# Scoring 24 of 128 expert tiles in the routing and table stages, and interleaving scores with outputs on TensorE

## What is computed

```python
q = (t @ wq).reshape(PEER_BLOCK, PEER_HEADS, 2, PEER_DQ // 2)
s1, s2 = einsum(q[:, :, 0], k1), einsum(q[:, :, 1], k2)
v1, i1 = lax.top_k(s1, 16); v2, i2 = lax.top_k(s2, 16)
score, ci = lax.top_k(v1[..., :, None] + v2[..., None, :], 16)
expert = i1[ci // 16] * 128 + i2[ci % 16]
g = softmax(score)
act = gelu(einsum('thkd,td->thk', u_tab[expert], t))
out = einsum('thk,thkd->td', g * act, v_tab[expert])
```

## Time and profile before

| | us |
|---|---|
| median of 3 runs (4811.25 to 4816.73) | 4812.54 |
| profiled execution | 4815.9 |
| its span, first to last instruction | 4814.1 |
| PE busy in it | 4348.4 (90%) |
| DVE busy | 2663.7 (55%) |
| ACT busy | 1814.3 (38%) |
| POOL busy | 526.0 (11%) |
| mean granted PE clock | 0.961 |

### The profile page before, as it was taken

How to read it: one execution, slowest core, us unless ns; L and a number is a source line. 1 busy time by engine, 2 the same in 40 slices (tenths; PEclk the granted TensorE clock), 3 DMA queues, 4 the chain that set the end, 5 groups by cost and what they waited for, 6 DMA issues and landing times. The chain is left out here.

```text
span 4814.1 us, 56280 instructions
## 1 busy us (share of the span) xinstructions
PE 4348.4 (90%) x20979; PEld 3540.2 (74%) x20979; DVE 2663.7 (55%) x4645; ACT 1814.3 (38%) x2539; POOL 526.0 (11%) x308
## 2 busy tenths in 40 slices
PE   8988888879998367999999997999999999999998
PEld 6866765646874256999999995777878877777887
DVE  0777758773437897767677675334343333434332
ACT  1665654443421033333333333345232233643322
POOL 0000000000003502334333430000000000000000
PEclk9999999989999699999999998999999999999999
DMA  7111101103322037887787771211323322122332
GB/s 263 58 40 44 40 31 49 43 1 108 92 63 67 5 140 281 281 279 270 282 278 276 274 273 65 70 53 59 99 88 97 96 84 70 51 77 84 102 97 81
DMA packets 196090, 579.09 MB, mean 120 GB/s; under 512 B 17345, under 2 KB 66753, under 8 KB 194369
## 3 DMA queue, kind: packets, MB, share of 16 engines
q1 hardware_dynamic: 158032, 435.34, 27.4%
q0 software_dynamic: 36864, 134.23, 7.9%
q10 hardware_dynamic: 1008, 7.03, 0.4%
HBM read 549.27 MB, written 27.26 MB: 120 GB/s over the span
## 5 line engine op out<-in xcount | busy, mean ns | idle before, releaser
L402 DVE TENSOR_TENSOR tile_rest<-tile_raw,tile_up 128x1024 fp32r<-128x1024 f32 (+2 forms) x288 | 338.7, 1181 | 786.4 <-ACT tile_up L393 786.2
L410 PE MATMUL layer_psum<-hn_up,tile_up 128*128 128x512 f32 x1344 | 534.7, 398 | 21.5 <-DVE hn_rest L497 21.5
L411 PE MATMUL layer_psum<-hn_up,tile_rest 128*128 128x512 f32 x1344 | 527.7, 393 | 0.0
L412 PE MATMUL layer_psum<-hn_rest,tile_up 128*128 128x512 f32 x1344 | 527.3, 392 | 0.0
L393 ACT ACTIVATE tile_up<-tile_raw 128x1024 fp32r<-128x1024 f32 (+2 forms) x288 | 291.4, 1018 | 370.3 <-PE layer_psum L412 368.5
L2205 PE MATMUL ex_psum<-ex_t_up,ex_u_up 128*128 128x384 f32 x1024 | 344.5, 336 | 9.1 <-ACT ex_prod L2280 4.9
L2207 PE MATMUL ex_psum<-ex_t_rest,ex_u_up 128*128 128x384 f32 x1024 | 344.4, 336 | 0.0
L2206 PE MATMUL ex_psum<-ex_t_up,ex_u_rest 128*128 128x384 f32 x1024 | 343.9, 336 | 0.0
L410 PEld LDWEIGHTS layer_psum<-hn_up,tile_up 128*128 128x128 f32 x1344 | 255.7, 190 | 82.4 <-issue 30.0
L2225 PE MATMUL ex_psum<-ex_v_up,ex_prod_rest 128*128 128x512 f32 x768 | 300.0, 391 | 0.0
L2223 PE MATMUL ex_psum<-ex_v_rest,ex_prod_up 128*128 128x512 f32 x768 | 299.9, 390 | 0.0
(11 more groups left out here) (450 smaller groups left out, 9981.3 us busy)
## 6 DMA issues: line engine op xcount, KB each, us to landing
ex_u<-in_peer_u SPq DMA_DIRECT2D x128, 512.0 KB, 4.3
tT<-in_peer_v SPq DMA_DIRECT2D x128, 512.0 KB
tile_raw<-in_w_gu SPq DMA_DIRECT2D x88, 512.0 KB, 3.6
xT<-in_w_head SPq DMA_DIRECT2D x56, 512.0 KB, 3.6
mod_w<-in_w_ada SPq DMA_DIRECT2D x48, 512.0 KB, 4.7
mg_w_raw<-in_w_merge SPq DMA_DIRECT2D x48, 512.0 KB
expert_table<-et_rows SPq DMA_DIRECT2D x6, 4096.0 KB
ex_rows<-expert_table SPq DMA_DIRECT2D x64, 384.0 KB, 6.2
```

The lines of the kernel that those rows point to most:

```text
L402: self.nc.vector.tensor_tensor(out=self.rest[:, n % self.SLOTS, 0:blocks, :], in0=self.raw[n % self.RAWS][:, 0:blocks, :], in1=self.up[:, ...
L410: self.nc.tensor.matmul(dst, w_up, up, start=first, stop=False)
L411: self.nc.tensor.matmul(dst, w_rest, up, start=False, stop=False)
L412: return self.nc.tensor.matmul(dst, w_up, rest, start=False, stop=last)
```

## The change

Every 5.33rd tile of the 128 (`EARLY`: 2, 8, 13, 18, 24, ... 125, 24 of them) is scored ahead of the experts stage, 12 in routing (behind the key scores of heads 1 to 7, one each and six behind the last) and 12 in the table stage (one matmul ahead of each of the 96 groups), in plain fp32 with 8 matmuls of 384 columns from u as it is, without cuts. ACT applies the gelu, SP writes 196 KB a tile to DRAM. In the experts stage SP reads these back where it would have loaded u. The other 104 tiles ("late") are numbered on their own; their buffers go by that number, scores alternate between two PSUM banks and wait for the gelu two late tiles back. PE now alternates the scores of one tile and the outputs of one tile. The loop of the experts stage is written out on all engines. In attention, 14 taps stand ahead of `a_rstd` in place of 8, and 4 in unit 0 in place of 10.

```diff
+EARLY = [(2 * k + 1) * NKEYS // 48 for k in range(24)]
+EARLY_ROUTING = 12
...
                 if i > 0:
-                    taps(8)
+                    taps(14)
                 dve.wait_ge(a_rstd, START + i + 1)
...
                     if u == 0:
                         rests_behind(plan.chain[i][:2])
-                        taps(10)
+                        taps(4)
                         rests_behind(plan.chain[i][2:])
...
+class EarlyScores:
+    SLOTS = 3
+
+    def __init__(self, ph, io, mem, banks, first, count):
+        self.u = [ph.sb(f"early_u{n}", [P, DB, P]) for n in range(self.SLOTS)]
+        self.out = [ph.sb(f"early_out{n}", [P, T_DENSE]) for n in range(2)]
...
+    def load(self, sp, e):
+        if e >= self.count:
+            return
+        if e >= self.SLOTS:
+            sp.wait_ge(self.scored, START + e - self.SLOTS + 1)
+        sp.dma_start(self.u[e % self.SLOTS][:],
+                     self.io["peer_u"][EARLY[self.first + e]]).then_inc(self.landed[e % self.SLOTS], 16)
+
+    def store(self, sp, e):
+        sp.wait_ge(self.gelu_ready, START + e + 1)
+        sp.dma_start(self.mem.early[self.first + e], self.out[e % 2][:]).then_inc(self.stored[e % 2], 16)
...
+    def block(self, nc, pe, e, d):
+        if d == 0:
+            pe.wait_ge(self.landed[e % self.SLOTS], START + 16 * (e // self.SLOTS) + 16)
+            if e >= 2:
+                pe.wait_ge(self.gelu_ready, START + e - 1)
+        ins = nc.tensor.matmul(self.banks[e % 2][:, 0:T_DENSE], self.u[e % self.SLOTS][:, d, :],
+                               self.mem.tT[:, d, 0:T_DENSE], start=d == 0, stop=d == DB - 1)
+        if d == DB - 1:
+            ins.then_inc(self.scored, 1)
+
+    def gelu(self, nc, act, e):
+        act.wait_ge(self.scored, START + e + 1)
+        if e >= 2:
+            act.wait_ge(self.stored[e % 2], START + 16 * (e // 2))
+        nc.scalar.activation(self.out[e % 2][:], self.banks[e % 2][:, 0:T_DENSE],
+                             ACT.Gelu_apprx_tanh).then_inc(self.gelu_ready, 1)
...
+        def early_of(h):
+            return range(0) if h == 0 else range(h - 1, h if h < HEADS - 1 else EARLY_ROUTING)
...
                     last.then_inc(s_filled, 1)
+                for e in early_of(h):
+                    for d in range(DB):
+                        early.block(nc, pe, e, d)
...
                 if h > 0:
                     weigh(h - 1)
+                for e in early_of(h):
+                    early.gelu(nc, act, e)
...
             for n in range(GROUPS):
+                early.block(nc, pe, n // DB, n % DB)
                 if n >= RING:
                     pe.wait_ge(unpacked, START + n - RING + 1)
...
+                if n % DB == DB - 1:
+                    early.gelu(nc, act, n // DB)
...
-            for s in range(2):
-                step(s, s % 2, s)
-            with eng.Fori(1, STEPS // 2 - 1) as i:
-                for par in range(2):
-                    step(i * 2 + par, par, None)
-            for s in range(STEPS - 2, STEPS):
+            for s in range(STEPS):
                 step(s, s % 2, s)
...
+                for j in range(s * G, s * G + G):
+                    if j in late:
+                        q = late[j]
+                        if q >= G:
+                            sp.wait_ge(u_cut, START + q - G + 1)
+                        sp.dma_start(u[q % G], io["peer_u"][j]).then_inc(u_landed[q % G], 16)
+                    else:
+                        k = soon[j]
+                        if k >= 2:
+                            sp.wait_ge(prod_cut, START + EARLY[k - 2] + 1)
+                        sp.dma_start(early[k % 2][:], mem.early[k]).then_inc(early_landed[k % 2], 16)
...
+            def scores(j):
+                q = late[j]
+                pe.wait_ge(u_cut, START + q + 1)
+                if q >= 2:
+                    pe.wait_ge(gelu_ready, START + q - 1)
+                dst = B[q % 2][:, 0:N]
...
+            def step(s, par, n):
                 for t in range(G):
+                    if (s + 1) * G + t in late:
+                        scores((s + 1) * G + t)
+                    outputs(s, par, t)
...
+                    if q >= 4:
+                        act.wait_ge(scored, START + q - 3)
+                    nc.scalar.activation(u_up[q % 4][:], u[q % G], ACT.Copy).then_inc(u_up_ready, 1)
...
+                    if j in late:
+                        dve.wait_ge(gelu_ready, START + late[j] + 1)
+                    else:
+                        dve.wait_ge(early_landed[soon[j] % 2], START + soon[j] // 2 * 16 + 16)
```

More of the change, by code:

```diff
@@ L2056, in phase_experts, with late_of @@
         pairs = [(par, t) for par in range(2) for t in range(G)]
+        late = {j: q for q, j in enumerate(j for j in range(NKEYS) if j not in EARLY)}
+        soon = {j: k for k, j in enumerate(EARLY)}
+        def late_of(s):
+            return [late[j] for j in range(s * G, s * G + G) if j in late]
         def ring(name, shape, dt=F32):
@@ L2072, in phase_experts @@
         own_v = {(0, 0): v_q[2], (0, 1): v_q[3], (1, 0): more_q[2], (1, 1): more_q[3]}
-        u_up, u_rest = ring("u_up", [P, DB, P], F32R), ring("u_rest", [P, DB, P], F32R)
+        u_up, u_rest = ([sb(f"{name}{n}", [P, DB, P], F32R) for n in range(4)] for name in ("u_up", "u_rest"))
+        early = [sb(f"early{n}", [P, N]) for n in range(2)]
         v_up, v_rest = ring("v_up", [P, DB, P], F32R), ring("v_rest", [P, DB, P], F32R)
@@ L2083, in phase_experts @@
         u_landed = [sem(f"u_landed{t}") for t in range(G)]
+        early_landed = [sem(f"early_landed{n}") for n in range(2)]
         v_landed = [sem(f"v_landed{t}") for t in range(G)]
@@ L2229, in step @@
-            def step(s, par, n):
-                if ahead(n, 1):
-                    scores(s + 1, 1 - par, later(n, 1))
-                outputs(s, par, n)
+            def scores(j):
[4 more added lines that the diff above has]
+                dst = B[q % 2][:, 0:N]
+                up, rest = u_up[q % 4], u_rest[q % 4]
+                for d in range(DB):
+                    nc.tensor.matmul(dst, up[:, d, :], t_up[:, d, :], start=d == 0, stop=False)
+                    nc.tensor.matmul(dst, rest[:, d, :], t_up[:, d, :], start=False, stop=False)
+                    last = nc.tensor.matmul(dst, up[:, d, :], t_rest[:, d, :], start=False, stop=d == DB - 1)
+                last.then_inc(scored, 1)
@@ new lines, in outputs @@
+            def outputs(s, par, t):
+                first, final = s * G + t == 0, s * G + t == NKEYS - 1
+                pe.wait_ge(v_cut, START + s * G + t + 1)
+                pe.wait_ge(prod_cut, START + s * G + t + 1)
+                for b in range(BLOCKS):
+                    cols = slice(b * P, (b + 1) * P)
+                    for half in range(2):
+                        rows = slice(half * DB // 2, (half + 1) * DB // 2)
+                        dst = total(b, half)
+                        nc.tensor.matmul(dst, prod_up[par, t][:, cols], v_up[par, t][:, rows, :], start=first,
+                                         stop=False)
+                        nc.tensor.matmul(dst, prod_up[par, t][:, cols], v_rest[par, t][:, rows, :], start=False,
+                                         stop=False)
+                        last = nc.tensor.matmul(dst, prod_rest[par, t][:, cols], v_up[par, t][:, rows, :],
+                                                start=False, stop=final)
+                if t == G - 1:
+                    last.then_inc(step_filled, 1)
@@ L2238, in _ @@
             pe.wait_ge(t_cut, START + DB)
-            scores(0, 0, 0)
+            for j in range(G):
+                scores(j)
             pe.wait_ge(own_t_ready, START + 2)
```

112 lines of the change are left out of this document (57 added, 55 removed).

## The result

The changed kernel takes **4692.09 us** (median of 4 runs, 4689.49 to 4692.70), beside 4814.64 us for the kernel before on the same chip: ratio 0.9745, 95% interval 0.9728 to 0.9762, 123 us less. The forecast was 4704 in a range of 4692 to 4746: right in direction and kind, and 12 us short, at the fast edge of the range. The ratio, applied to the 4812.54 us that the forecast started from, gives 4689.8, 2 us outside the range. The profiled execution took 4692.7 us with a span of 4690.9.

What follows compares the result with a forecast made beforehand. PE was taken to bound the experts stage, busy throughout its steady part. The terms -100.1 + 2 + 4 + 0 + 2 - 18 sum to -110.1 us, 4702.4 from the median; forecast 4704 us, range 4692 to 4746.

Steps and rivals of the forecast that it cites:

- Experts: Experts stage: 24 of 128 tiles lose their scores on PE, 4.17 us each, -100.1 us; charges of +2 and +4 beside it.
- Transfers: Experts stage: early steps need 348 GB/s, as the busiest step shows; charged +2 us, bounds 0 and +70.
- rival 2: Experts stage: transfers bind in early steps, 15.4 us at 280 GB/s, not 12.4; +72 us, 4776, half of it 4740; chance 0.13.
- The start: Start of experts: tile 2 early leaves PE idle 8 us before first outputs, then half clock; +4 us, bounds 0 and +8.
- The alternation: Experts steps: second score tile ends 4 us later, but results are due a step later, so PE does not wait: 0.
- Routing 0, table +2: Early scoring fits PE's idle time: routing 0 (bounds -1, +6); table +2 us for its start (bounds 0, +62).
- Unrolling: Experts loop written out: PE shows no gap at the loop's turns, so removing them brings 0.
- Rivals 1: Table stage: early matmul misses the wait, groups take 1.75 us or more; +12 us (4716) to +60 (4764); chance 0.09.
- 3: Unrolled experts stage: 40 more instruction packets, each exposed by 0.9 us; +36 us, 4740; chance 0.05.
- 4: Attention: taps bring nothing, since ACT's cut in unit 0 comes as late; 4722 us; chance 0.06.
- 5: Table stage: PE falls to 1.2 GHz, a group takes 3.14 us instead of 1.63; +145 us, 4849; chance 0.02.
- Taps: Attention's four passes: moved taps give back PE's idle before unit 1 and DVE's before a_rstd; -18 us, bounds -24 and -5.

Runs made afterwards that it cites:

- early_shifted: The changed kernel with tile 4 early in the place of tile 2: 4691.01 us, ratio 0.9748.
- early_12: The changed kernel with 12 early tiles, all in routing and none in the table stage: 4744.47 us, ratio 0.9858.
- unrolled_only: The kernel before with the steps of the experts stage unrolled, nothing else: 4815.85 us, ratio 1.0002.
- taps_14_4: The kernel before with only the taps edit, dealt 14 and 4: 4784.07 us, ratio 0.9939.

## Why the prediction was right and where it failed

**Experts, -94.1 forecast, -93.3 measured.** Right, partly by terms that cancel. 4.17 us a tile was right (4.15 and 4.08). Transfers, charged +2, cost nothing as the tiles are dealt: the steady part has PE busy throughout at 297 GB/s. Early steps in sequence did cost 2.3 us each, where rival 2 had 3, but as that trace reads by a wait of SP's queue for a buffer, a path that the prediction did not name, and not by the rate that rival 2 was about. The start, charged +4, cost 4.3 by early_shifted, with the wait of 8 us where it was placed. The alternation, put at 0 because the results are due a step later, costs 4.1 us without early tiles and 2.7 in the changed kernel (40 full steps, by 0.067 us each): the argument looked at waits, while the cost lies in the turns themselves, of which the earlier trace rows show only the old number, so that zero should have been one end and not the value.

**Routing 0, table +2.** Measured 0 and +2.2, by early_12. **Unrolling 0**: right, with 36 instruction packets on q8 in the steady part (1 in the earlier trace rows) and PE without a gap there. What the Trainium skill's "Runtime: NRT & Kernel Launch" (Instruction fetch mechanics) says of block crossings, mostly hidden, agrees with unrolled_only. The ACT switches of routing cost DVE's heads nothing. "ScalarE: Activation LUTs" (Rules for kernel authors) in the Trainium skill budgets some 2.7 us for a switch. The rows above do not agree: the copy ends at 1497.39 and the exponential behind the load starts at 1498.70, 1.31 us later, so the 14 switches took the 18 us of the prediction and not the 38 by the page. Rivals 1, 3, 4 and 5 did not happen either: the groups stayed at 1.63 us, and PE's clock in the table stage was 0.98.

**Taps, -18 with bounds -24 and -5: the step that failed.** The idle part was right: unit 1's transposes start 4.3, 4.2, 4.2 and 4.6 us sooner in their passes, 17.3 us, against "up to 4.7 us in each". The step said of the half clock behind the idle "some 2 us, of which DVE's pace lets little through". Counted by stretches, changed against before, passes one to three gain another 0.6, 3.0 and 0.7 us between unit 1 and the mean, 1.7, 1.6 and 1.6 us from the mean to the next pass, and pass four 0.6: 9.8 us that the sum did not hold. The experiments split it. The first part is the clock behind the idle and belongs to the taps. The second, 4.9 us here, is the clock at the mean: the sum had nothing for it, the kernel before had it low behind passes one to three, and with PE's waits unchanged it was full behind passes one and three of the changed kernel, while behind pass two the eight records took 4.66 us instead of 6.30. The taps' own 20.5 us lie inside the bounds, and the clock at the mean carried the passes beyond them. That it came with the taps in pass one is shown; how much of it will come in passes two and three is not, and there the changed kernel was lucky beside taps_14_4.

**The rest.** Another 4.5 us came from stages behind the experts, whose executions spread over 1884.6 to 1892.0 us. Forecast sum -110.1 against -123.2 in the profile: taps 9.1, rest 4.5, experts -0.8, elsewhere 0.3. Without the last stretch and the mean's clock the profile's own time would have been 4702 us (123.2 - 4.5 - 4.9 = 113.8 below 4815.9); the range had no term for either, and a gain of 123 us fell on its edge. The 4.5 us are chance as far as the runs show, since the repeat of the changed kernel had only 0.7 of them.

## What to carry to other kernels

Price an idle gap of TensorE as the gap plus the slow records behind it, look for other places in the same stage whose clock is already at half, and give the range a term for that clock. Deal shortened steps out among full ones, or give what they read enough buffers: a queue that is worked in order and waits for a free buffer delays every load behind it. Work moved ahead of a wait must also have its own input by then, or it holds up what stands behind it in the queue.

## What the runs showed that was not expected

- The same eight matmul records behind the same 2.27 us wait took 4.97 us in one kernel and 3.27 in another, without an edit near them; with two unread matmuls ahead of them they took 3.27 us in all three passes of all three kernels that had this fill. The same instructions also differ between kernels whose edits lie elsewhere.
- Five matmuls a pass whose result nobody reads made a kernel no slower, and two a pass made it 0.17% faster (interval 0.08 to 0.26%).
- A turn between the two matmul streams of the experts stage (384 columns by u, 512 columns by v) costs about 0.03 us each with every operand ready.
